# Projection and sliding attention turned round in a one-layer hybrid encoder step

## The reference, cut to what matters

```python
p = rmsnorm(x, g) @ w_in        # 1024 prompt rows and 64 sample rows, 1024 -> 2312 columns
q_a, k_a, v_a, f_a, q_b, k_b, v_b = split(p, [512, 512, 512, 8, 512, 128, 128])
logf = log_sigmoid(f_a + b_forget)
# (A) forgetting attention, 8 heads of 64, causal, plus cumulated log-forget bias
o_a = softmax(q_a @ k_a.T * SCALE + c_q - c_k) @ v_a
# (B) sliding attention, 8 query heads on 2 key heads, 128 back, ALiBi, learned sinks
o_b = sink_softmax(q_b @ k_b.T * SCALE + alibi) @ v_b
x = x + concat(rmsnorm(o_a), rmsnorm(o_b)) @ w_out
x = x + moe(rmsnorm(x))         # top-2 of 32 experts, gated MLP 1024 -> 128 -> 1024
y = rmsnorm(x)                  # k_a, v_a, logf and the last k_b, v_b are outputs too
```

## Time and profile before

| | us |
|---|---|
| median of 3 runs (lowest, highest) | 956.46 (955.55, 960.39) |
| the profiled execution's own time | 959.17 |
| its span | 957.3 |
| TensorE busy, weight loads | 829.1 (87%), 716.0 |
| VectorE busy | 459.7 (48%) |
| ScalarE busy | 331.6 (35%) |
| mean granted TensorE clock | 0.944 of full speed |
| chain that ended last, by engine | PE 75%, DVE 11%, ACT 5%, DMA 4%, issue 4% |

### The profile page before, as it was taken

One profiled execution on the slowest core, in us unless ns is written; L12 is line 12 of the kernel. 1 busy time (PEld: TensorE's weight loads), 2 busy tenths in 40 slices (PEclk: granted clock), 3 DMA queues, 4 the chain that ended last, 5 costly groups with the idle time before them and its releaser, 6 DMA issues.

```text
span 957.3 us, 16435 instructions
## 1 busy us (share of the span) xinstructions
PE 829.1 (87%) x6131; PEld 716.0 (75%) x6131; DVE 459.7 (48%) x1142; ACT 331.6 (35%) x837; POOL 82.9 (9%) x138
## 2 busy tenths in 40 slices
PE   4999999999979889899999799999299999999500
PEld 3999999999957666677888588887276777777300
DVE  4731110111156656555776454663437555444377
ACT  5531111101146566655666343232022222222123
POOL 0000000000000000000000000000323334443100
PEclk9999999999979999999999799999589999999855
DMA  8211114110450411005000421120988999972195
GB/s 265 92 31 45 45 44 135 45 44 31 68 166 23 53 37 26 2 1 221 2 2 2 178 89 65 68 78 23 377 291 333 343 323 331 339 285 80 54 387 183
DMA packets 62498, 124.61 MB, mean 130 GB/s; under 512 B 13387, under 2 KB 34723, under 8 KB 62435
## 3 DMA queue, kind: packets, MB, share of 16 engines
q1 hardware_dynamic: 53219, 105.91, 32.9%
q0 software_dynamic: 9216, 17.85, 5.2%
HBM read 108.72 MB, written 30.73 MB: 146 GB/s over the span
## 4 chain that ended last, share of the span: by engine, by line
PE 75%; DVE 11%; ACT 5%; DMA 4%; issue 4%; SPq 0%; POOLq 0%; DVEq 0%; POOL 0%; ACTq 0%
PE ps L1517 34%; PE ps L1865 11%; PE ps L1871 5%; PE ps L1744 4%; PE ps L1858 3%; PE ps L1626 2%; DVE big L1124 2%; PE ps L1610 2%; PE ps L1720 2%; PE ps L1731 2%; PE ps L1641 2%; PE ps L1804 2%; ACT big L757 1%; DMA out_y_prompt<-big 1%; PE ps L1682 1%
## 5 line engine op out<-in xcount | busy, mean ns | idle before, releaser
L1517 PE MATMUL ps<-wg_hi,xl 128*128 128x256 f32 x576 | 163.4, 284 | 0.3 <-DVE wg_lo L996 0.3
L1517 PE MATMUL ps<-wg_hi,xh 128*128 128x256 f32 x576 | 163.0, 283 | 0.0
L1517 PE MATMUL ps<-wg_lo,xh 128*128 128x256 f32 x576 | 163.0, 283 | 0.0
L1517 PEld LDWEIGHTS ps<-wg_hi,xl 128*128 128x128 f32 x576 | 110.5, 192 | 0.5 <-issue 0.5
L1517 PEld LDWEIGHTS ps<-wg_lo,xh 128*128 128x128 f32 x576 | 110.6, 192 | 0.0
L1517 PEld LDWEIGHTS ps<-wg_hi,xh 128*128 128x128 f32 x576 | 110.5, 192 | 0.0
L1865 PEld LDWEIGHTS ps<-fox,work 128*128 128x128 f32 x320 | 60.6, 190 | 19.4 <-issue 12.2
L1865 PE MATMUL ps<-fox,work 128*128 128x256 f32 x320 | 72.5, 379 | 2.0 <-DVE work L1415 2.0
L1415 DVE COPY work<-ps 128x512 f32<-128x512 f32 x32 | 22.1, 692 | 94.8 <-PE ps L1858 94.7
L1000 DVE COPY fox<-ps 128x256 f32 (+1 forms) x27 | 11.4, 422 | 101.8 <-PE ps L1517 101.8
L1517 PE MATMUL ps<-w_out_h,oTl 128*128 128x512 f32 x144 | 58.9, 409 | 1.5 <-DVE oTl L1258 1.5
(11 more groups left out here) (295 smaller groups left out, 1770.1 us busy)
## 6 DMA issues: line engine op xcount, KB each, us to landing
fox<-in_w_gate SPq DMA_DIRECT2D x20, 512.0 KB, 4.6
fox<-in_w_up SPq DMA_DIRECT2D x20, 512.0 KB, 6.3
fox<-in_w_down SPq DMA_DIRECT2D x20, 512.0 KB, 6.5
work<-in_w_in SPq DMA_DIRECT2D x8, 1024.0 KB, 5.5
fox<-y_rows SPq DMA_DIRECT2D x16, 512.0 KB, 7.1
h_rows<-big SPq DMA_DIRECT2D x9, 512.0 KB, 2.7
work<-in_x_prompt SPq DMA_DIRECT2D x8, 512.0 KB, 4.6
fox<-in_w_out SPq DMA_DIRECT2D x1, 4096.0 KB, 14.0
```

The costliest lines, as they stand in the source:

```text
L1517: mm = pe.matmul(out, xs[a](c), ws[b](c), start=(c + k == 0), stop=(c == C - 1 and k == 2))
```

## The change

Weights are held still and tokens streamed for the queries of both attentions and for the forgetting keys, so these come out with the head dimension on partitions and need no staging. The order of the groups is now v, v, sliding k and v (as before, tokens on partitions), then k, k, q, q, sliding q, sliding q (turned: six units of 384, 384 and 320 tokens, twice). A group's sliding q is loaded as four DMAs, so that one head of each key head lie together. The forgetting keys are also an output with tokens on partitions: nine times four turns (`turn_k`) in groups 5 to 7, ScalarE copies them to one buffer (`copy_k`), SP sends each. The high and low parts of a pair are now made in two bursts (tiles 0 to 3, and 4 to 8 with the cache) from SBUF. In the sliding attention V is held still, the result is copied by ScalarE and turned back by TensorE (`sback`). At the experts' start the first four gathers use the table in place, and slots 4 to 6 are loaded only after the first two gathers have landed.

```diff
+        G_AT = [1024, 1280, QKV + NH + 512, 512, 768, 0, 256]
+        TURNED = 3
+        U0 = [NT * g if g <= TURNED else NT * TURNED + 6 * (g - TURNED) for g in range(NG + 1)]
+        T0 = [0, 3, 6, NT]
+        KO_AT = {U0[5] + 2 * i + 1: i for i in range(NT)}
-            return ([(0, 2 + i)] if it == 0 and i < 4 else []) + ([(it + 1, i - 3)] if it + 1 < NH // 2 and i >= 3 else [])
+            return [(it + 1, (i - 3) // 2)] if i in (3, 5) and it + 1 < NH // 2 else []
+        PARTS = [(0, 4), (4, NT)]
+        S_AT = {3: 0, 6: 1}
...
             for g in range(1, NG):
                 if g >= 3:
-                    sp.wait_ge(s["proj_done"], NT * (g - 1))
+                    sp.wait_ge(s["proj_done"], U0[g - 1])
+                if g < 7:
+                    sp.dma_start(wg_raw[g % 2], wg_cols(g)).then_inc(wg_in[g % 2], 16)
+                else:
+                    for j in range(2):
+                        for u in range(2):
+                            c0 = QKV + NH + (4 * u + 2 * (g - 7) + j) * DH
+                            sp.dma_start(wg_raw[g % 2][:, :, (2 * j + u) * DH:(2 * j + u + 1) * DH],
+                                         w_in_dram[:, :, c0:c0 + DH]).then_inc(wg_in[g % 2], 16)
+                for i in {6: (0, 1), 7: (2, 3, 4), 8: (5, 6, 7, 8)}.get(g, ()):
+                    send_k(i)
...
-            for k in range(2, NSLOT - 1):
+            for k in range(2, 4):
+                expert(k)
+            for k in range(2):
+                sp.wait_ge(g_in[k], 16)
+            for k in range(4, NSLOT - 1):
                 expert(k)
...  ScalarE
+            for g in range(1, NG):
+                for k in units(g):
+                    if k == U0[g] + (3 if g < TURNED else 1) and g + 1 < NG:
+                        act.wait_ge(s["proj_done"], U0[g])
+                        high_w((g + 1) % 2, W_LOADS[g + 1])
+                    if k % 2:
+                        evac(g, k)
+                    if k - 2 in KO_AT:
+                        copy_k(KO_AT[k - 2])
+            def fsplit(it, part):
+                a, b = PARTS[part]
...
+                act.activation(kh[it % 2][:, a:b, :], k_raw[:, it, a:b, :], ACT.Copy)
+                if part:
+                    act.activation(kh[it % 2][:, NT:NK, :], ck_T[:, it, :, :], ACT.Copy)
+                act.activation(qh[it % 2][:, a:b, :], q_raw[:, it, a:b, :], ACT.Copy, scale=SCALE).then_inc(s["st_hi"], 1)
+            def s_copy_o(n):
+                act.wait_ge(s["s_pv"], n + 1)
+                act.wait_ge(s["oN_done"], NF + n)
+                act.activation(oTs, bank[6][:, 0:P], ACT.Copy).then_inc(s["oT_cp"], 1)
...          (step n, after scopy(n) and before the w_out row)
+                if n >= 1:
+                    s_copy_o(n - 1)
...  VectorE: flow(it, part) is the low half of fsplit, after both its copies
-                dve.wait_ge(s["s_pv"], n + 1)
+                dve.wait_ge(s["oN_done"], NF + n + 1)
...          (step n, after smax(n + 2))
-                if n >= 1:
-                    snorm(n - 1)
+                if n >= 2:
+                    snorm(n - 2)
...  TensorE
+                    j, tg = divmod(k - U0[g], 3)
+                    cols, toks = slice(j * P, (j + 1) * P), slice(T0[tg] * P, T0[tg] * P + unit_width(g, k))
+                    mm = three_passes(out, (lambda c: wg_hi[u][:, c, cols], lambda c: wg_lo[u][:, c, cols]),
+                                      (lambda c: xh[:, c, toks], lambda c: xl[:, c, toks]))
+            def turn_k(i):
...
+                if i:
+                    pe.wait_ge(s["ko_set"], i)
+                for it in range(NH // 2):
+                    mm = pe.transpose(bank[0][0:rows, it * P:(it + 1) * P], k_raw[:, it, i, 0:rows], ident)
...
+                        mm = pe.matmul(bank[6][v * DH:v * DH + DH, 0:P], val, sprobT[n % 2][:, (2 * v + b) * P:(2 * v + b + 1) * P],
+            def sback(n):
+                pe.wait_ge(s["oT_cp"], NF + n + 1)
                 pe.wait_ge(s["s_od"], n + 1)
+                pe.transpose(bank[7][:, 0:P], oTs, ident).then_inc(s["oN_done"], 1)
...
                 strans(n)
+                if n >= 2:
+                    sback(n - 2)
                 if n + 2 < NW:
                     sqk(n + 2)
```

More of the change, by code:

```diff
@@ L713, in _ @@
             act.activation(lz[:, 2 * n:3 * n], lz[:, n:2 * n], ACT.Ln, bias=eps[:, 1:2]).then_inc(s["lf_s"], 1)
-            def group(n0, k0, loads, proj, dest, more=True):
-                for i in range(NT):
-                    if i == 3 and more:
-                        act.wait_ge(s["proj_done"], proj)
-                        high_w((k0 + 1) % 2, loads)
-                    if (k0 + i) % 2:
-                        evac(n0 + i, k0 + i, dest(i))
-            with act.Fori(0, 2) as j:
-                for g in (1, 2):
-                    group(j * 2 * NT + g * NT, g * NT, j + (g + 2) // 2, j * 2 * NT + g * NT,
-                          lambda i: fox_t[:, i, ds(j * 2 * WG + g * WG, WG)])
@@ L745, in _, with copy_k @@
-            for i in range(NT):
-                n = (NG - 1) * NT + i
-                if n % 2:
-                    evac(n, n, wg_dest(NG - 1, i))
-            high(0, 0, 0)
-            high(0, 1, 1)
+            def copy_k(i):
+                rows = P if i < SAMPLE else DEC
+                act.wait_ge(s["ko_T"], i + 1)
+                if i:
+                    act.wait_ge(s["ko_out"], 16 * i)
+                act.activation(k_out[0:rows, :], bank[0][0:rows, :], ACT.Copy).then_inc(s["ko_set"], 1)
@@ L1154, in _, with s_low_k @@
                     fmax(n + 1, 1)
-                for it, g in staged_at(n):
-                    low(it, g)
+                for it, part in split_at(n):
+                    flow(it, part)
             fnorm(NF - 2)
             fnorm(NF - 1)
-            def s_low(n, first, end, b, key):
-                dve.wait_ge(s["s_hi"], n + 1)
-                src = bank[b][:, 0:(end - first) * P].rearrange("p (t k) -> p t k", k=P)
-                if not key:
-                    dve.scalar_tensor_tensor(out=sql[:, first:end, :], in0=src, scalar=SCALE, in1=sqh[:, first:end, :].bitcast(F32),
-                                             op0=ALU.mult, op1=ALU.subtract).then_inc(s["s_lo"], 1)
-                    return
+            def s_low_k(n, first, end, b):
+                dve.wait_ge(s["s_hi"], 2 * n + 1)
                 if end > NT:
@@ L1649, in fback @@
                     pe.wait_ge(s["o_done"], n)
-                pe.wait_ge(s["st_lo"], 2 + sum(len(staged_at(m)) for m in range(min(n + 2, NF))))
                 pe.transpose(bank[7][:, 0:P], oTs, ident).then_inc(s["oN_done"], 1)
@@ L1660, in _ @@
                 fturn(n, 1)
-                if n >= 1:
+                if n == 0:
+                    pe.wait_ge(s["cache_in"], 64)
+                else:
                     fpv(n - 1)
-                for it, g in staged_at(n):
-                    stage(it, g, backs=max(n - 1, 0))
             fback(NF - 2)
```

417 lines of the change are left out of this document (208 added, 209 removed).

## The result

The changed kernel takes 950.99 us (median of 5 runs, 950.80 to 952.79), the kernel before 956.46 (5 runs, 954.92 to 960.39). The ratio is 0.9944, 95% interval 0.9923 to 0.9965: faster by 0.35 to 0.77%. Predicted were 947 and a range of 934 to 960. The profiled execution took 950.99 (span 949.2) against 959.17, so 8.2 less where 9.2 was forecast. Much of this agreement is luck: one stage is 7.6 worse than predicted, another 0.9, and three are better.

What follows compares the result with a forecast made beforehand. TensorE bounds projection and sliding attention, a circle of waits the forgetting attention, the first gather the experts' start. Terms -4.2 - 1.6 + 0.2 - 3.6 = -9.2 give 950.0 of its own, 947 against the median; range 934 to 960.

Steps and rivals of the forecast that it cites:

- Projection, -4.2: Projection: longer matmuls -13.1, added turns +4.0, waits for weights in small pieces +4.9, together -4.2 us.
- The waits: Projection: TensorE's key turns wait for ScalarE behind 256 B weight loads landing in 8.1; 2.4 per group, +4.9 in all.
- rival 1: Projection: a 256 B piece costs what a 1 KB piece does, 52 ns; +19.4 for +4.9, kernel 962; chance 0.10.
- Forgetting attention, -1.6: Forgetting attention: start +1.5, staging of the first pair gone -4.0, next pairs' bursts +0.9, together -1.6 us.
- The later pairs: Forgetting attention: about 4.0 of staging waits goes per pair, two bursts come; net +0.3, three times.
- the price of the bursts: Forgetting attention: ScalarE and VectorE work on the two bursts costs 1.2 and 3.1 us per pair after hiding.
- Rival 3: No change: bursts cost 1.5 more per pair (+4.5), the first gather is not quicker (+3.6); 955 us; chance 0.25.
- Sliding attention, +0.2: Sliding attention: start -0.8, query turns -7.9, VectorE copy waits -2.0, `w_out` rows +9.3, query parts +1.6, together +0.2 us.
- The circle: Sliding attention: `sqk`, `smax`, `snorm`, `sback` wait on one another, setting a step of 2.28, so `spv`'s saving is given back.
- The `w_out` steps: Sliding attention: ScalarE's row waits behind the result copy, delaying VectorE; steps of 3.5, 1.2 lost in each of eight, +9.3.
- Rival 2: Much faster: TensorE stays the bound in sliding steps of 1.96 and `w_out` rows hide; -19.9, kernel 927; chance 0.15.
- Experts' start, -3.6: Experts' start: first gather 4.3 instead of 7.57 with fewer loads before it, index copy of 0.3 gone; -3.6 us.

Runs made afterwards that it cites:

- the later parts: High and low parts of the two last projection weight groups formed two units later, against the kernel at 919.01: 916.24 us.
- the five edits together: Changed kernel plus five small parts, lows one step later, `snorm` before `smax`, idle matmuls at the changeover, `w_out` high parts on GpSimd; V held still: 919.01 us.
- the experiment: Changed kernel with both experts' start edits undone: all expert weights issued before the first gathers, indices of the first four gathers copied: 956.94 us.
- the fastest version: The kernel at 919.01 with high and low parts of the two last projection weight groups formed two units later: 916.24 us.

## Why the prediction came out

- *Projection, -4.2, was -7.1.* Turned groups of 23.8 (-13.1) and 0.44 per four turns (+4.0) hold. The waits were sized 4.9 and are about 2.1 (0.85 + 1.3). Two experiments take them away: 2.25 with pieces of 1 KB and 1.55 with the later parts, each against its own base; in the profiles that have the waits the projection ends anywhere from 253.6 to 254.4, so this is as near as they can agree. The mechanism and the place were right; the landing was 7.0 and 7.5, not 8.1, and TensorE had 0.44 of turns more to do meanwhile than was counted. With the prediction's 2.1 of latency a 256 B piece took some 19 to 21 ns of an engine (an estimate: 4.9 and 5.4 us over 256 pieces), nearer its low end of 17 than its high end of 52: rival 1 is excluded. (The count of added turns is 36, not 37; the sum stays +4.0.)
- *Forgetting attention, -1.6, was +6.0: the step that failed.* Start: +2.3; without the late decay rows 6.93 - 5.43 = 1.5, as forecast, and 0.8 for their landing, a load whose wait the prediction had not looked for. It was issued 1.4 later than before the change (240.31 for 238.92), behind the last new store of K, and took 20.4 instead of 18.6. First pair: -2.1 for -4.0. The later pairs: +0.3 each was forecast, and about +2 came (5.8 in all). The term that failed is the price of the bursts, 1.2 + 3.1 per pair from "VectorE waits for both ScalarE copies, so nothing overlaps inside a burst"; it measured 1.8 and 4.6 to 5.8. It counted the burst's own two engines' work and not what ScalarE has ahead of its part, an exponential of 1.15 and the copy; nor that the idle time would halve the clock, for which it had 1.1 at the start and nothing here. That TensorE's idle time in the second burst is 3.06, as the term said, is luck: with the lows one step later the same copies cost 0.1 to 1.1 and 1.1 in these two places and 0.6 one step on, so it is the wait that costs and not the sum of the copies. That edit took 14.5 off. Rival 3 had bursts at +1.5 per pair, near the +1.6 that came, but gave no mechanism, and its other half (a gather that is not quicker) is wrong.
- *Sliding attention, +0.2, was +1.1.* The circle is right, 2.38 for 2.28, with each member within 0.11, and moving one call to break it gives 2.09 (TensorE's own 1.96 was estimated; `spv` is 0.59 for 0.47, `strans` 0.59 for 0.45, `sback` 0.12 for 0.25). The `w_out` steps are 3.31 for 3.5, in the order that the prediction named; with V moving they are 2.28 and cost nothing. What it missed is the changeover: without the turns of the queries TensorE idles, and the clock is at half to 441.7. From the first scores to the fifth tile's it takes 2.35 more than before the change. That took back the start's 0.8 and more.
- *Rival 2* (TensorE the bound, -20) was wrong for the kernel as written and comes near for one a few lines away: with `snorm` first TensorE is the bound, at steps of 2.09 and not 1.96, and with the five edits together the sliding stretch is 16.8 shorter.
- *Experts' start, -3.6, was -5.0*, of which 2 to 4 are the edit's by the experiment; the first gather landed in the 4.3 of the prediction. What the rest is stays open.
- *Sum.* -9.2 of its own was forecast and -8.2 came, of which 3.1 is the wait at the end of the one execution before, which I take for chance. Medians differ by 5.5, and the changed kernel's is 4.0 above the 947 of the forecast. The forecast held because errors of +7.6 and +0.9 met others of -2.9, -1.4 and -3.1.

What stays open: why the clock came back after 7 us in one kernel and not for some 150 in half the executions of the other, with TensorE at work in both; and how much of the 40 us of the fastest version each of its edits gives when the others are there, since only some were run alone.

## What to carry to other kernels

When work is gathered into bursts on two engines that follow one another, ask at the place in both lists when each engine reaches its part; here the wait was the first one's backlog there, smaller parts only multiplied it, and putting the second part a step later removed it. When an edit takes work out of TensorE's list at a changeover, ask what is left to keep it at work: some 2.8 us idle out of 5 cost about 2 in clock in one kernel, and 60 in three of six executions of another. A circle of waits through three engines is worth a try of each order of two neighbouring calls before anything is rebuilt.

## What the runs showed of the hardware

- The granted clock stayed at half, 1.2 GHz, for some 150 us under a TensorE that was busy 30.00 of 30.00, after 5 us in which it was busy 2.28. It did so in three of six executions (3 at about 1003, 3 at about 940), the same program each time.
- 1 MB in four DMAs of 256 B pieces lands in 6.8 to 7.5 (three profiles), in one of 1 KB pieces in 5.5 and 5.6.
- GpSimd rounds 128x1024 float32 in 1.04, the same as ScalarE's 1.05. VectorE's rows of 128x128 with two inputs take 0.292 beside such a copy and without it.
